# Two-block transformer kernel, MLP: the odd parts' up activations turned by sixteen VectorE transposes

## The chip, the cores and the metric

One core of a Trainium2 chip runs the whole program. The metric is the device time of one execution in microseconds (us); for the kernel before it is the median of three runs.

## The reference, cut to what matters

Two transformer blocks run on 256 tokens of width 2048 in float32. The change lies in the MLP of the first block only, which is

```python
h = rmsnorm(x, norm_mlp_g[l])
x = x + jnp.square(jax.nn.relu(h @ w_up[l])) @ w_down[l]      # 2048 -> 8192 -> 2048
```

## The kernel before, in words

Every float32 weight is split into a high and a low fp32r part, so that a product is three TensorE products (high x high, low x high, high x low). Weights come in **units** of 128 x 1024 numbers (512 KB). SyncE loads a unit into one of four slots of `w_raw`, ScalarE copies it rounded to `w_hi` (`split`, line 1273), VectorE subtracts to get `w_lo` (`split`, line 1989), and TensorE runs twelve 128 x 512 products on it (`token_unit`, line 636). ScalarE and VectorE work four units ahead: in step `j` of their loops they split unit `j + 4`, which ScalarE may do once TensorE is through with unit `j`, because it takes the same slot.

The MLP is cut into 16 parts of 512 hidden columns. A part's up projection is a chunk of 8 units; its down projection is 4 chunks of 2 units, one for each 512 output columns. Two PSUM sets take turns from chunk to chunk. After a chunk, VectorE adds the set to `x` (`add_tokens`, line 2004, two instructions) and so frees it; the down chunks are 2 units long, so that the set is wanted again two units after the chunk's end. Seven passes of one loop, counted 0 to 6 here, do two parts each in 32 steps: units 0 to 7 up (part `2i+1`), 8 to 15 down (part `2i`), 16 to 23 up (part `2i+2`), 24 to 31 down (part `2i+1`). The adds stand in steps 9, 11, 13, 15, 25, 27, 29 and 31.

TensorE's up products have the tokens on the partitions; the down products want the hidden columns there. So a part's activations are turned: ScalarE applies relu and square (lines 1469 and 1472, in step 7 for the odd part, semaphore `hid_sq`), VectorE transposes the blocks of 32 x 32 in place of quadrants by one instruction (`turn_blocks`, line 2338, step 10), and ScalarE moves the sixteen groups of blocks to their quadrants of 32 partitions (`move_blocks`, shown in the profile at line 1273 as `arena<-arena 32x256`, two in each of steps 11 to 18). Then ScalarE and VectorE make the high and the low part (`moved_hi` in step 20, `moved_lo` in step 21, line 2343), on which the down units wait (`hid_ready`).

The same VectorE queue also multiplies the modulation weights of the second block (`ada`, line 1984, `arena<-arena,cs 128x768`) in every step of 0 to 23 but each third. Step 28 sums them up (`partial_sums`, `modulation`). GpSimd builds tables beside this; its three stages are released by `hid_ready` (waits on line 3144 and after), so they begin after a `moved_lo`.

Engines take their instructions strictly in the order of the code. The feed-forward stage of the second block already turns its product in quadrant pieces on VectorE (`turn_product`, line 2941), two in each of eight steps.

Of the kernel before, what the change touches and what calls it, by code (L numbers as in the profile page):

```python
# [38 lines left out]
FT = COLS // P  # L39
# [249 lines left out]
def two_blocks(nc, a, consts, columns, x_by_dim, s5_in, s5_blocks, small_in, wide_in2, out):  # L289
# [5 lines left out]
    sem = {n: ctx.enter_context(nc.semaphore(n)) for n in SEMS}  # L295
# [56 lines left out]
    def vec(name, i=0, n=1):  # L352
        g, r, k = VEC[name]
        return vecs[:, g * P + r + i:g * P + r + i + n]

    def T(t, n=None):
        return arena[:, t, :] if n is None else arena[:, t:t + n, :]

    def flat(ap):
        return ap.rearrange("p a b -> p (a b)")  # L360
# [41 lines left out]
    def span(t, off, n):  # L402

        return arena[:, :, :].rearrange("p a b -> p (a b)")[:, t * S + off:t * S + off + n]
# [15 lines left out]
    HID_B, HID_T = 4, 8  # L420
# [6 lines left out]
    def by_block(tiles):  # L427

        return flat(tiles).rearrange("p (t f g b) -> p t f g b", t=TT, f=FT, g=QUADS)

    def by_feature(tiles):

        return tiles.rearrange("p f (t g b) -> p t f g b", t=TT, g=QUADS)

    def quad(q):

        return slice(q * QUAD, (q + 1) * QUAD)
# [833 lines left out]
    def _(act):  # L1271
        def copy(o, i, scale=1.0):
            return nc.scalar.activation(o, i, ACT.Copy, scale=scale)  # L1273

        def split(R, j, first=False, cols=COLS):

            act.wait_ge(raw_landed[j % RAW], (R * (8 // RAW) + j // RAW) * 16 + 16)
            if not first:
                act.wait_ge(sem["unit_done"], R * 8 + (j - LEAD + 1))
            copy(w_hi[:, j % LEAD, :, 0:cols], w_raw[:, j % RAW, :, 0:cols]).then_inc(sem["hi_ready"], 1)  # L1280
# [6 lines left out]
        def halves(ap):  # L1287
            return ap.rearrange("p (a b) -> p a b", a=2)
# [67 lines left out]
        for b in range(KT // 2):  # L1356
# [3 lines left out]
            for k in range(2 * b, 2 * b + 2):  # L1360
                m = copy(hop_hi[:, k], T(XT + k), scale=vec("norm_mix_g", k))
# [72 lines left out]
        for j in range(4 * UA):  # L1434
# [16 lines left out]
            for c in range(3):  # L1451
                if j == OUT_LAST[c] + 1:
                    i = OUT_GROUPS.index((c, 1))
# [20 lines left out]
        def move_blocks(m, first, n):  # L1474

            act.wait_ge(sem["hid_turned"], m + m + 1)
            for k in range(first, first + n):
                q, g = k // QUADS, k % QUADS
                i = copy(by_feature(T(HID_T, FT))[quad(g), :, :, q], by_block(T(HID_B, FT))[quad(q), :, :, g])
            if first + n == QUADS * QUADS:  # L1480
                i.then_inc(sem["hid_turned"], 1)

        def moved_hi(par, m):

            act.wait_ge(sem["hid_turned"], m + m + 2)
            copy(hid_hi[:, par], T(HID_T, FT)).then_inc(sem["hid_hi"], 1)
# [22 lines left out]
        with act.Fori(0, MLP_SUPER // 2 - 1) as i:  # L1509
            for j in range(4 * UA):  # L1510
                split(R_MLP + 1 + 4 * i, j + LEAD)
                if j in (4, 20):
                    moved_hi(j // 20, 2 * i + j // 20)
                if j < 3:
                    move_blocks(2 * i, 10 + 2 * j, 2)
                if 11 <= j < 19:
                    move_blocks(2 * i + 1, 2 * (j - 11), 2)
                if 27 <= j < 32:
                    move_blocks(2 * i + 2, 2 * (j - 27), 2)
                if j == 7:  # L1520
                    hidden_relu(1, H_MLP + 5 * i, 2 * i + 1)
                if j == 23:
                    hidden_relu(0, H_MLP + 5 * i + 3, 2 * i + 2)
# [140 lines left out]
        for h in range(BR_HEADS):  # L1664
            c = 4 + h
            for q in range(UA):
                projection_unit(c, q)
                wide_lo(c, q)
                if q in (1, 2):
                    m = q - 1  # L1670
                    act.wait_ge(sem["d_negmax"], 2 * h + m + 1)
                    e = span(34, CW * m, CW)
                    for qt, cols in enumerate((slice(0, P), slice(P, CW))):
                        i = nc.scalar.activation(e[:, cols], e[:, cols], ACT.Exp, bias=st[:, 0, 2 * m + qt:2 * m + qt + 1],
                                                 accum_out=st[:, 1, 2 * m + qt:2 * m + qt + 1])
# [37 lines left out]
        for h in range(BR_HEADS):  # L1713
            c = 8 + h
            for q in range(UA):
# [10 lines left out]
                if h == 0 and q == 1:  # L1726
                    act.wait_ge(sem["g_z_psum"], 1)
                    for t in range(2):
                        m = nc.scalar.activation(T(8 + t), PS[4][:, t * S:(t + 1) * S], ACT.Identity, bias=vec("gla_ba_2", t))
                    m.then_inc(sem["g_z"], 1)  # L1730
                    head_root(0, 34)
                if q == 3:
# [3 lines left out]
                    for qt, cols in enumerate((slice(0, P), slice(P, CW))):  # L1736
                        m = nc.scalar.activation(e[:, cols], e[:, cols], ACT.Exp, bias=st[:, 0, 2 + qt:3 + qt])
# [74 lines left out]
        for i in range(4):  # L1812
            source = (0, 4, 0, 24)[i]
            for j in range(40):
# [8 lines left out]
                if j % 10 == 7:  # L1823
                    n = j // 10
# [10 lines left out]
                    for t in range(TT):  # L1835
                        m = nc.scalar.activation(flat(o)[:, t * COLS:(t + 1) * COLS], SETS[0][t][:], ACT.Sigmoid)
# [4 lines left out]
                if i == 3 and j in (13, 23, 33):  # L1841
                    n = j // 10 - 1
                    act.wait_ge(sem["merged_turned"], n + 1)
                    act.wait_ge(sem["hid_ready"], MLP_SUPER + 4)
                    for b in range(2):
                        m = copy(T(16 + FT * n + 2 * b, 2), halves(PS[5 + b][:]))
# [7 lines left out]
        def mix_square(c, t, junk):  # L1854

            return nc.scalar.activation(junk, SETS[c % 2][t][:], ACT.Square, accum_out=sums[:, SUM_MIX, t, c:c + 1])
# [10 lines left out]
        for j in range(4 * UA - LEAD):  # L1867
# [5 lines left out]
            if j % UA == UA - 1:  # L1873
                c = j // UA
                for t in range(TT):
                    m = mix_square(c, t, span(24, t * COLS, COLS))
# [64 lines left out]
        R, m = R_FFN + 2 + 6 * PAIRS, 2 * PAIRS + MLP_SUPER  # L1941
# [31 lines left out]
    def _(dve):  # L1973
        V = nc.vector
# [98 lines left out]
        for b in range(KT // 2):  # L2073
            dve.wait_ge(sem["hop_hi"], 2 * (b + 1))
            for k in range(2 * b, 2 * b + 2):
                m = stt(hop_lo[:, k], T(XT + k), vec("norm_mix_g", k), hop_hi[:, k].bitcast(F32), ALU.mult, ALU.subtract)
# [176 lines left out]
        for j in range(8 * UA):  # L2253
# [16 lines left out]
            if j == 12:  # L2270
                token_inverse(1, SUM_X)
                dve.wait_ge(sem["const_in"], 16)
                for t in range(TT):
                    m = V.tensor_scalar(span(46, t * P, P), ident, inverse(SUM_X, t), None, ALU.mult)
# [60 lines left out]
        def turn_blocks(m):  # L2335

            dve.wait_ge(sem["hid_sq"], m + 1)
            V.transpose(flat(T(HID_B, FT)), flat(T(0, FT))).then_inc(sem["hid_turned"], 1)  # L2338

        def moved_lo(par, m):  # L2340

            dve.wait_ge(sem["hid_hi"], m + 1)
            V.tensor_tensor(hid_lo[:, par], T(HID_T, FT), hid_hi[:, par].bitcast(F32), ALU.subtract).then_inc(sem["hid_ready"], 1)

        turn_blocks(0)
        with dve.Fori(0, MLP_SUPER // 2 - 1) as i:
            R, H = R_MLP + 1 + 4 * i, H_MLP + 5 * i
            for j in range(4 * UA):
                split(R, j + LEAD)
                if j in (5, 21):  # L2350
                    moved_lo(j // 21, 2 * i + j // 21)
                down_ends(R, j, 8, 0, x_tok)
                down_ends(R, j, 24, 1, x_tok)
                ada(ADA_ONE, j, i + G_MLP)
                if j in (10, 26):
                    turn_blocks(2 * i + (1 if j == 10 else 2))
                if j == 28:
                    partial_sums(i + G_MLP)
                    modulation(i + G_MLP)
# [36 lines left out]
        for j in range(3 * UA - LEAD):  # L2396
# [11 lines left out]
            if j in (17, 19):  # L2408
                n = j // 19
                dve.wait_ge(drained[n], H_IN2)  # L2410
                for t in range(TT):
                    m = gained(t, n)
# [90 lines left out]
        for j in range(3 * UA + SMALL_UNITS):  # L2503
# [7 lines left out]
            if 4 <= j < 8:  # L2511
                c = j - 4
                for t in range(TT):
                    m = V.tensor_scalar(x_tok[:, t, part(c)], Y_TOK[:, t, part(c)], inverse(SUM_MID, t), None, ALU.mult)
# [124 lines left out]
        for h in range(BR_HEADS):  # L2639
            for q in range(UA):  # L2640
# [16 lines left out]
                if h == 2 and q == 5:  # L2657
# [5 lines left out]
                    for t in range(2):  # L2663
                        m = V.tensor_tensor_scan(run[:, t, 1:S + 1], ones[:, 0:1].to_broadcast([P, S]), la[:, t], 0.0,
                                                 ALU.mult, ALU.add)
# [140 lines left out]
        for i in range(4):  # L2806
            R, H = R_GATE + 5 * i, H_GATE + 4 * i
            source = (0, 4, 0, 24)[i]
            for j in range(40):
# [7 lines left out]
                if j % 10 == 9:  # L2817
                    n = j // 10
# [3 lines left out]
                    for b in range(2):  # L2822
                        m = V.tensor_tensor(sig[:, 2 * b:2 * b + 2], halves(SETS[1][b][:]), sig[:, 2 * b:2 * b + 2], ALU.mult)
# [39 lines left out]
        for j in range(4 * UA - LEAD):  # L2863
# [14 lines left out]
            if j % UA == UA - 1:  # L2878
# [3 lines left out]
                for t in range(TT):  # L2882
                    m = gained_mix(c, t)
# [381 lines left out]
```

## Time and profile before

| what | value |
|---|---|
| median of 3 runs | 2606.64 us (2604.88 to 2607.6) |
| the profiled execution | 2607.81 us |
| its span | 2605.8 us |
| TensorE products (PE) busy | 2570.9 us, 99% |
| VectorE (DVE) busy | 2023.2 us, 78% |
| ScalarE (ACT) busy | 1360.8 us, 52% |
| granted TensorE clock | 0.997 of full |

The span is the time between the first and the last instruction of the profiled execution. Busy shares are of the span; matmuls overlap one another, so their busy time is not that of TensorE at its peak. Which engine ends the waits of the others is read from the rows on single stretches.

### The profile page before, as it was taken

The numbers are of one execution on the slowest core, as the hardware profiler recorded it, in microseconds if no ns is written. First come the engines' busy times: TensorE is split into PE (matmuls) and PEld (weight loads), VectorE is DVE, ScalarE is ACT, GpSimd is POOL, SyncE is SP. The second block draws the span as 40 slices with busy tenths as digits, with TensorE's granted clock in tenths as the row PEclk, the third lists the DMA queues.
The fourth block names the chain that finished last, engine by engine and source line by source line (L and its number), as shares of the span: only waits on it lengthen the run. The fifth ranks groups of instructions, "written<-read, shape, count | busy, mean of one in ns | idle before, by whom it ended". The sixth has DMA issues, their size and how long they took to land.

```text
span 2605.8 us, 35123 instructions
## 1 busy us (share of the span) xinstructions
PE 2570.9 (99%) x12360; PEld 2145.7 (82%) x12360; DVE 2023.2 (78%) x2572; ACT 1360.8 (52%) x1774; POOL 277.3 (11%) x309
## 2 busy tenths in 40 slices
PE   9999999999999999999999999999999999999998
PEld 8998888888878887888888877888788888888886
DVE  5798778888888879876676888787866666666798
ACT  6445565656565656455556444444544444444444
POOL 0021042233222000071000000000000000000000
PEclk9999999999999999999999999999999999999999
DMA  9666687879787886756555766789566666666785
GB/s 314 225 209 228 223 284 254 275 259 310 248 281 262 306 274 212 277 170 222 170 173 162 258 226 212 240 304 323 181 202 193 193 193 193 193 193 193 258 298 187
DMA packets 284076, 611.10 MB, mean 235 GB/s; under 512 B 20400, under 2 KB 21620, under 8 KB 282048
## 3 DMA queue, kind: packets, MB, share of 16 engines
q1 hardware_dynamic: 279104, 583.54, 68.6%
q0 software_dynamic: 4864, 26.14, 2.8%
q8 instruction: 66, 1.08, 0.2%
q14 instruction: 42, 0.34, 0.0%
HBM read 599.08 MB, written 11.29 MB: 234 GB/s over the span
## 4 chain that ended last, share of the span: by engine, by line
PE 87%; DVE 7%; issue 3%; ACT 3%; DMA 1%; DVEq 0%; SPq 0%; ACTq 0%
PE ps L636 86%; DVE w_lo L1989 1%; DVE arena L1984 1%; ACT w_hi L1273 1%; DMA w_raw<-in_w_in 1%; DVE x L2004 0%; DVE hop_part L1984 0%; PE ps L756 0%; DVE arena L2941 0%; DMA w_raw<-in_ffn_w_out 0%; ACT hop_part L1273 0%; PE ps L777 0%; DVE arena L2004 0%; DVE mod_parts L2115 0%; DVE x L1984 0%
## 5 line engine op out<-in xcount | busy, mean ns | idle before, releaser
L1273 ACT ACTIVATE w_hi<-w_raw 128x1024 fp32r<-128x1024 f32 (+1 forms) x898 | 948.1, 1057 | 1153.1 <-PE ps L636 1040.8
L1989 DVE TENSOR_TENSOR w_lo<-w_raw,w_hi 128x1024 fp32r<-128x1024 f32 x809 | 1014.2, 1255 | 476.1 <-ACT w_hi L1273 472.3
L636 PE MATMUL ps<-w_hi,hop_part 128*128 128x512 f32 x4264 | 1334.5, 391 | 3.4 <-DVE w_lo L1989 1.5
L636 PEld LDWEIGHTS ps<-w_hi,hop_part 128*128 128x128 f32 x4264 | 800.7, 188 | 178.1 <-issue 8.3
L636 PE MATMUL ps<-w_lo,hop_part 128*128 128x512 f32 x2132 | 829.8, 389 | 0.0
L636 PEld LDWEIGHTS ps<-w_lo,hop_part 128*128 128x128 f32 x2132 | 400.5, 188 | 81.4
L636 PE MATMUL ps<-w_hi,hid_hi_part 128*128 128x512 f32 x992 | 387.5, 391 | 2.8 <-DVE x L2004 2.7
L636 PE MATMUL ps<-w_hi,hid_lo_part 128*128 128x512 f32 x992 | 386.0, 389 | 0.0
L636 PE MATMUL ps<-w_lo,hid_hi_part 128*128 128x512 f32 x992 | 386.0, 389 | 0.0
L636 PE MATMUL ps<-hop_part,w_hi 128*128 128x256 f32 (+1 forms) x1312 | 275.3, 333 | 5.8 <-DVE hop_part L1984 5.8
L1984 DVE SCALAR_TENSOR_TENSOR arena<-arena,cs 128x768 f32<-128x768 f32 x240 | 254.7, 1061 | 0.3
L636 PEld LDWEIGHTS ps<-hop_part,w_hi 128*128 128x128 f32 x1312 | 216.5, 194 | 25.1 <-issue 7.6
L636 PEld LDWEIGHTS ps<-w_hi,hid_hi_part 128*128 128x128 f32 x992 | 186.2, 188 | 45.0 <-issue 6.3
L636 PEld LDWEIGHTS ps<-w_hi,hid_lo_part 128*128 128x128 f32 x992 | 186.2, 188 | 38.8
L636 PEld LDWEIGHTS ps<-w_lo,hid_hi_part 128*128 128x128 f32 x992 | 186.3, 188 | 38.1
L636 PE MATMUL ps<-hop_part,w_lo 128*128 128x256 f32 x912 | 176.6, 284 | 0.0
L2489 DVE TENSOR_TENSOR w_lo<-w_raw,w_hi 128x1024 fp32r<-128x1024 f32 x84 | 106.1, 1267 | 61.9 <-ACT w_hi L1273 61.6
L636 PEld LDWEIGHTS ps<-hop_part,w_lo 128*128 128x128 f32 x912 | 143.7, 192 | 5.2
L1273 ACT ACTIVATE arena<-arena 32x256 f32<-32x256 f32 x240 | 99.8, 416 | 19.3 <-DVE arena L2338 15.4
L2004 DVE TENSOR_TENSOR x<-ps,x 128x512 f32<-128x512 f32 x124 | 79.3, 680 | 0.0
L3173 POOL DMA_DIRECT2D gain_scratch<-arena x2 | 1.0, 520 | 678.8 <-ACT arena L1273 678.8
L636 PE MATMUL ps<-arena 64*128 64x128 f32 (+4 forms) x496 | 69.3, 342 | 3.8 <-DVE arena L2177 2.9
(320 smaller groups left out, 1424.2 us busy)
## 6 DMA issues: line engine op xcount, KB each, us to landing
arena<-in_ada_w SPq DMA_DIRECT2D x256, 384.0 KB, 5.1
w_raw<-in_ffn_w_in SPq DMA_DIRECT2D x176, 512.0 KB, 3.7
w_raw<-in_w_up SPq DMA_DIRECT2D x128, 512.0 KB, 4.2
w_raw<-in_w_down SPq DMA_DIRECT2D x128, 512.0 KB, 4.8
w_raw<-in_w_gate SPq DMA_DIRECT2D x128, 512.0 KB, 4.3
w_raw<-in_ffn_w_out SPq DMA_DIRECT2D x88, 512.0 KB, 3.6
w_raw<-in_w_in SPq DMA_DIRECT2D x87, 512.0 KB, 4.3
w_raw<-in_w_out SPq DMA_DIRECT2D x64, 512.0 KB, 5.5
```

Source lines behind the costliest of these rows:

```text
L636: return nc.tensor.matmul(o, w, r, start=start, stop=stop, skip_group_check=True)
L1273: return nc.scalar.activation(o, i, ACT.Copy, scale=scale)
L1984: return V.scalar_tensor_tensor(o, i0, scalar, i1, op0, op1, **k)
L1989: V.tensor_tensor(w_lo[:, j % LEAD, :, 0:cols], w_raw[:, j % RAW, :, 0:cols], w_hi[:, j % LEAD, :, 0:cols].bitcast(F32), ALU.subtract).the ...
L2004: m = V.tensor_tensor(at[:, t, part(c)], SETS[s][t][:], at[:, t, part(c)], ALU.add)
L2489: V.tensor_tensor(w_lo[:, slot], w_raw[:, slot], w_hi[:, slot].bitcast(F32), ALU.subtract).then_inc(sem["lo_ready"], 1)
L3173: pool.dma_start(gain_scratch[i].rearrange("(k p) -> k p", p=P), gain_rows[32 + 32 * i:32 + 32 * i + KT, :]).then_inc(sem["scratch_out"], 16)
```

## The change

In steps 10 to 17 of the loop, VectorE issues two transposes of 32 partitions x 256 elements after whatever else the step holds. Each reads one quadrant of the squared activations `T(0, FT)` and writes the quadrant of `T(HID_T, FT)` to which the blocks belong. The one block instruction of step 10 and ScalarE's sixteen moves in steps 11 to 18 go. The last piece raises `hid_turned` by 2, for the block instruction and for the last move. The even parts keep the old way (`turn_blocks` in step 26, `move_blocks` in steps 27 to 31 and 0 to 2 of the next pass), as does the part before the loop, and the last part is turned by TensorE as before. Nothing on TensorE, SyncE or GpSimd changes.

```diff
@@ ScalarE's loop
                 if j < 3:
                     move_blocks(2 * i, 10 + 2 * j, 2)
-                if 11 <= j < 19:
-                    move_blocks(2 * i + 1, 2 * (j - 11), 2)
                 if 27 <= j < 32:
                     move_blocks(2 * i + 2, 2 * (j - 27), 2)
@@ VectorE
+        def turn_piece(m, n):
+
+            dve.wait_ge(sem["hid_sq"], m + 1)
+            q = n // 2
+            for g in range(2 * (n % 2), 2 * (n % 2) + 2):
+                i = V.transpose(by_feature(T(HID_T, FT))[quad(g), :, :, q], by_block(T(0, FT))[quad(q), :, :, g])
+            if n == 7:
+                i.then_inc(sem["hid_turned"], 2)
@@ VectorE's loop
                 ada(ADA_ONE, j, i + G_MLP)
-                if j in (10, 26):
-                    turn_blocks(2 * i + (1 if j == 10 else 2))
+                if j == 26:
+                    turn_blocks(2 * i + 2)
+                if 10 <= j < 18:
+                    turn_piece(2 * i + 1, j - 10)
```

On VectorE, steps 10 to 13 of the loop stand like this before (each step begins with the `w_lo` row; `x<-ps,x` is the add of a chunk, `arena<-arena,cs` the modulation product):

```order
L1989 TENSOR_TENSOR w_lo<-w_raw,w_hi 128x1024
L2108 REGISTER_ALU
L1984 SCALAR_TENSOR_TENSOR arena<-arena,cs 128x768
L2337 REGISTER_ALU
L2338 STREAM_TRANSPOSE arena<-arena 128x1024
L1988 REGISTER_ALU
L1989 TENSOR_TENSOR w_lo<-w_raw,w_hi 128x1024
L2004 TENSOR_TENSOR x<-ps,x 128x512 x2
L1988 REGISTER_ALU
L1989 TENSOR_TENSOR w_lo<-w_raw,w_hi 128x1024
L2102 ISA
L2108 REGISTER_ALU
```

The changed kernel has, from the same `w_lo` row of step 10 on:

```order
L1987 TENSOR_TENSOR w_lo<-w_raw,w_hi 128x1024
L2106 REGISTER_ALU
L1982 SCALAR_TENSOR_TENSOR arena<-arena,cs 128x768
L2340 REGISTER_ALU
L2343 STREAM_TRANSPOSE arena<-arena 32x2x4x32 x2
L1986 REGISTER_ALU
L1987 TENSOR_TENSOR w_lo<-w_raw,w_hi 128x1024
L2002 TENSOR_TENSOR x<-ps,x 128x512 x2
L2343 STREAM_TRANSPOSE arena<-arena 32x2x4x32 x2
L1986 REGISTER_ALU
L1987 TENSOR_TENSOR w_lo<-w_raw,w_hi 128x1024
```

One large transpose in step 10 has become a pair of small ones there and a pair behind the add of step 11; further pairs close each step up to 17, so that three pairs stand ahead of the add of step 13.

On ScalarE, the steps from 11 on before:

```order
L1273 ACTIVATE w_hi<-w_raw 128x1024
L1476 REGISTER_ALU
L1273 ACTIVATE arena<-arena 32x2x4x32 x2
L1277 ISA
L1279 REGISTER_ALU
L1273 ACTIVATE w_hi<-w_raw 128x1024
L1273 ACTIVATE arena<-arena 32x2x4x32 x2
```

and in the changed kernel:

```order
L1273 ACTIVATE w_hi<-w_raw 128x1024
L1277 ISA
L1279 REGISTER_ALU
L1273 ACTIVATE w_hi<-w_raw 128x1024
L1279 REGISTER_ALU
L1273 ACTIVATE w_hi<-w_raw 128x1024
```

The moves between the high splits are gone, and with them the wait for `hid_turned` that stood ahead of the first of them.

## Rows read from the trace of the kernel before

**Rows 1.** The page, busy time of each engine: engine, busy us (share) xinstructions.

```profile
PE   2570.9 (99%) x12360; PEld 2145.7 (82%) x12360; DVE 2023.2 (78%) x2572; ACT 1360.8 (52%) x1774; POOL 277.3 (11%) x309
```

**Rows 2.** Stretches: sum us, busy PE, PEld, DVE, ACT, POOL, PEclk, DMA share, GB/s.

```profile
441.76:465.49 23.73, 22.36 (x98) 17.87 (x96) 23.73 (x22) 13.94 (x19) 9.64 (x6) 1.00 0.88 316
531.34:553.10 21.76, 21.76 (x97) 18.02 (x96) 20.71 (x22) 13.94 (x19) 6.23 (x5) 1.00 0.85 280
574.86:596.62 21.76, 21.76 (x97) 18.02 (x96) 21.35 (x27) 13.94 (x19) 10.55 (x7) 1.00 0.75 258
618.38:640.14 21.76, 21.76 (x97) 18.02 (x96) 20.68 (x22) 13.94 (x19) 20.03 (x35) 1.00 0.86 280
```

**Rows 3.** Timeline of PE, pass 1: start us, us, instruction [idle before <-releaser].

```profile
452.41 0.39 PE L636 MATMUL ps<-w_hi,hid_lo_part 128*128 128x512 f32 x1
453.45 0.49 PE L636 MATMUL ps<-w_hi,hid_hi_part 128*128 128x512 f32 x1 [0.65 <-DVE x L2004]
453.78 0.39 PE L636 MATMUL ps<-w_lo,hid_hi_part 128*128 128x512 f32 x1
```

**Rows 4.** Timeline of DVE: adds of steps 9, 11, 13 of pass 1, 13 of pass 3.

```profile
452.05 1.27 DVE L2004 TENSOR_TENSOR x<-ps,x 128x512 f32<-128x512 f32 x2
...
458.50 1.27 DVE L2004 TENSOR_TENSOR x<-ps,x 128x512 f32<-128x512 f32 x2
...
462.94 1.28 DVE L2004 TENSOR_TENSOR x<-ps,x 128x512 f32<-128x512 f32 x2
...
637.34 1.27 DVE L2004 TENSOR_TENSOR x<-ps,x 128x512 f32<-128x512 f32 x2
```

**Rows 5.** Groups: busy us, mean ns of one, idle ahead: the ScalarE moves.

```profile
L1273 ACT ACTIVATE arena<-arena 32x256 f32<-32x256 f32 x240 | 99.8, 416 | 19.3 <-DVE arena L2338 15.4
```

**Rows 6.** Timeline of DVE, feed-forward stage: pieces in steps without idle time.

```profile
2446.40 1.23 DVE L1989 TENSOR_TENSOR w_lo<-w_raw,w_hi 128x1024 fp32r<-128x1024 f32 x1 [0.36 <-ACT w_hi L1273]
2447.54 0.87 DVE L2941 STREAM_TRANSPOSE arena<-arena 32x256 f32<-32x256 f32 x2
2448.43 0.62 DVE L2106 TENSOR_SCALAR arena<-arena,cs 128x768 f32<-128x768 f32 x1
2449.12 1.23 DVE L1989 TENSOR_TENSOR w_lo<-w_raw,w_hi 128x1024 fp32r<-128x1024 f32 x1
2450.37 0.89 DVE L2941 STREAM_TRANSPOSE arena<-arena 32x256 f32<-32x256 f32 x2
2451.28 1.02 DVE L1984 SCALAR_TENSOR_TENSOR arena<-arena,cs 128x768 f32<-128x768 f32 x1
```

**Rows 7.** Timeline of DVE, pass 2: steps 10, 11 and 13.

```profile
543.40 1.24 DVE L2338 STREAM_TRANSPOSE arena<-arena 128x1024 f32<-128x1024 f32 x1
544.57 1.18 DVE L1989 TENSOR_TENSOR w_lo<-w_raw,w_hi 128x1024 fp32r<-128x1024 f32 x1
545.67 1.28 DVE L2004 TENSOR_TENSOR x<-ps,x 128x512 f32<-128x512 f32 x2
...
550.10 1.28 DVE L2004 TENSOR_TENSOR x<-ps,x 128x512 f32<-128x512 f32 x2
551.30 1.01 DVE L1984 SCALAR_TENSOR_TENSOR arena<-arena,cs 128x768 f32<-128x768 f32 x1
552.22 1.22 DVE L1989 TENSOR_TENSOR w_lo<-w_raw,w_hi 128x1024 fp32r<-128x1024 f32 x1
```

**Rows 8.** Timeline of DVE, pass 2: step 21, then 23 to 25, then 29.

```profile
570.71 1.23 DVE L1989 TENSOR_TENSOR w_lo<-w_raw,w_hi 128x1024 fp32r<-128x1024 f32 x1 [1.50 <-ACT w_hi L1273]
...
577.62 6.29 DVE L1989 TENSOR_TENSOR w_lo<-w_raw,w_hi 128x1024 fp32r<-128x1024 f32 x3
583.83 1.27 DVE L2004 TENSOR_TENSOR x<-ps,x 128x512 f32<-128x512 f32 x2
...
594.95 1.28 DVE L2004 TENSOR_TENSOR x<-ps,x 128x512 f32<-128x512 f32 x2
```

**Rows 9.** DMA issues in the loop, 325 to 1000 us: KB each, us to landing.

```profile
w_raw<-in_w_up SPq DMA_DIRECT2D x116, 512.0 KB, 4.2
```

## Prediction

> **What bounds the kernel now.** I read the busy times first: TensorE's products fill 99% of the span, VectorE's work 78% [rows 1]. So the change can only matter where TensorE waits, or comes to wait, in the stretch it touches. The second view is the table of stretches [rows 2]. Its first, third and fourth columns of time show the length, TensorE's and VectorE's work. Eight units take TensorE 21.76 us when nothing disturbs it, 2.72 us a unit, at a granted clock of 1.00. In the down units of step 8 to 15 VectorE is busy 20.71 of 21.76 us in pass 2 and 20.68 in pass 3; in pass 1 it is busy for the whole stretch, and the stretch has grown to 23.73 us (pass 4 reads the same). So here VectorE stands a few tenths of a us behind the bound, while ScalarE has 8 us to spare (13.94 of 21.76).
>
> The third view is the timeline around the two waits of pass 1 [rows 3, 4]. The product at 452.41 us should be followed 0.23 us later, at 452.64, but the next begins at 453.45, and the profile names the add to x as releaser. The add of step 9 began at 452.05 and took 1.27, so ended at 453.32. The product behind the wait is a long one (0.49 in place of 0.39), and the next comes at 453.78, as if the first had begun at 453.55. So a chunk costs TensorE nothing as long as the add that frees its PSUM set ends 0.23 us ahead of its start, and each us later costs a us. Here the loss is 453.32 + 0.23 - 452.64 = 0.91 us. The add of step 11 ended at 459.77; two units behind 453.55 is 458.99, so it cost 1.01. Together 1.92, and the stretch is 1.97 longer: the rule accounts for it.
>
> What reaches the end of the program is therefore the end of the adds. In pass 2 the add of step 13 begins at 550.10 [rows 7] and ends at 551.38, and unit 16, which wants its set, starts at 553.10: it has 1.72 - 0.23 = 1.49 us to spare.
>
> **What the change removes.** ScalarE loses 16 moves of 416 ns in each of seven passes [rows 5], 46.6 us. I price this at nothing: with 8 us of 21.76 idle, ScalarE is behind TensorE's release of a slot, not ahead of it. VectorE loses one block transpose in each pass. From its start to that of the step 11 add are 2.27 us, with one split between [rows 7]; a split is 1.14 us from start to start [rows 6], so the block transpose is worth 1.13.
>
> **What it adds.** The feed-forward stage has the same pieces, in a place without idle time [rows 6]. The first pair, 2447.54 to 2448.43, holds VectorE for 0.89 us, and the split ahead of it keeps its 1.14. The second stands 1.25 us behind its split's start, and the next instruction 0.91 after the pair's: the split's end no longer overlaps what follows, which is 0.11 more. So the first pair (both pieces read quadrant 0, the first also writes it) costs 0.89, every other 0.91 + 0.11 = 1.02. These rows show the 0.11 behind a split alone; in steps 11 to 13 the pairs stand behind an add or a modulation product. Those two also overlap their followers: an add takes 1.28 and the next starts after 1.20, a product 1.01 and 0.92 [rows 7]. I take 1.02 there too; the other bound is 0.91.
>
> By the Trainium skill, page "VectorE: DVE Perf Modes", section "Two Vector instructions with no wait between them", an instruction that starts in another quadrant than the last one read or wrote is held until all earlier ones have finished. By it the sum is the one below, since every pair but the first is held whatever stands ahead of it; were it held behind splits alone, the sum would be the second case's. Rows 6 agree with it, 1.14 us behind a split for the first pair and 1.25 for the next.
>
> **The add of step 13.** The pair in step 10 replaces the block transpose: the add of step 11 starts 0.89 + 1.14 = 2.03 us after it, 0.24 earlier. Then two more pairs, 2.04, stand ahead of the add of step 13, so it comes 1.80 us later. In pass 2: 550.10 + 1.28 + 1.80 + 0.23 = 553.41 against 553.10, a loss of 0.31 where there was none. I take passes 0, 5 and 6 like it: 1.24. In pass 3 the add starts at 637.34 and takes 1.27 [rows 4]; with 2.03 more that is 640.64 against 640.14 [rows 2], 0.50. In passes 1 and 4 the loss at step 11 shrinks by 0.24, unit 16 would start at 465.49 - 0.24 = 465.25, and the add of 462.94 ends at 464.22, with 2.03 more 466.25: 1.00 lost, 0.76 net; 1.52 for both. The add of step 15 has a whole chunk of 8 units to spare. Sum: 1.24 + 0.50 + 1.52 = 3.26 us.
>
> **The splits behind it.** All eight pairs cost 0.89 + 7 x 1.02 = 8.03. From the start of step 10's pair to that of step 17's split stand seven pairs (7.01), six splits (6.84), three adds (3.60) and four modulation products (3.68): 21.13 us. In pass 2 that split starts at 564.53, its result counts from 564.53 + 1.23 + 0.23 = 565.99, and unit 21 is due at 553.41 + 5 x 2.72 = 567.01. One us is left; the loads stay covered too: unit 25's, released by it at 565.76, lands 4.2 us later [rows 9], 569.96, and ScalarE has until 571.95 to split it, when VectorE comes for it (next part).
>
> **What VectorE takes on into the second half.** From the block transpose (543.40) to step 21 (570.71) are 27.31 us [rows 7, 8]. The work in them is 2.27 + nine splits 10.26 + three adds 3.60 + six products 5.52 = 21.65, so 5.66 are idle. The change adds 8.03 - 1.13 = 6.90, and 1.24 stay over. Most passes lose that in idle stretches behind it. Not passes 2 and 5: there GpSimd begins its longest step after `moved_lo`, and the three splits of steps 23 to 25 take 6.29 us in place of 3.4, with no idle time up to the add of step 25 [rows 8]. That add ends at 583.83 + 1.27 + 1.24 + 0.23 = 586.57 by the rule; unit 28 is due at 574.86 + 10.88 + 0.31 = 586.05: 0.52 lost. The add of step 29 comes to 596.23 + 1.24 + 0.23 = 597.70 against 596.62 + 0.31 + 0.52 = 597.45, 0.25 more. Two passes: 1.54 us.
>
> **Sum.** 3.26 + 1.54 = 4.8 us more. The profiled execution took 2607.81 us and would take 2612.6; the median of the runs is 1.17 below it, so 2606.64 + 4.8 = 2611.4 us, 0.18% more. A measurement of this kernel can tell about 0.2%, or 5.2 us, from no change.
>
> **The rivals.**
>
> First, *pairs held only behind splits*. Pairs in steps 11 and 12 cost 0.91, the add of step 13 is 0.22 earlier: losses of 0.09 in four passes, 0.28 in pass 3, 0.54 in passes 1 and 4, 1.72 in all. VectorE keeps 5 x 0.11 less, 0.69; the adds of steps 25 and 29 then lose 0.19 and 0.25, twice 0.44. Total 2.6, so 2609.2 us. For it: I have no row of a pair behind an add. Against: each piece in rows 6 but the first starts after its forerunner's full duration.
>
> Second, *slower: GpSimd stretches the pieces too*. Pass 3 has it busy for 20.03 of 21.76 us [rows 2], pass 0 is in the same stage of the tables. Were pieces stretched as the splits of rows 8, 6.29 / 3.42 = 1.84 times, three pairs ahead of the step 13 add would be 3 x 0.89 x 0.84 = 2.2 us longer, in two passes 4.5: 9.3 in all, 2615.9 us. It decides against "no difference" from 0.2 us in each of the two passes on. Against: the add of pass 3 takes 1.27 us [rows 4], as in pass 1 where GpSimd has finished, so not every VectorE instruction is stretched. A late load ends on the same side: one that takes over a us longer than in rows 9 shifts steps 21 to 25 of passes 2 and 5 by the rest.
>
> Third, *faster, by ScalarE's freedom*. ScalarE waited 15.4 us for the block transposes [rows 5]; without that its splits come earlier. But TensorE lost only 1.97 us in such a stretch, to adds, not to splits, and all that the change can return there is 0.24 us in each of two passes if the step 13 add still fits: 2606.2 us. Faster by over 0.2% has no source.
>
> **How the numbers follow.** The forecast, 4.8 us with its own spread of 3.5 to 6.5, has 50%; pairs held only behind splits or mostly hidden (under 3.5) 24%; stretched pieces or late loads (over 6.5) 24%; faster 2%. The range of 8 in 10 goes from 2608.3, just under the second case, to 2615.9, the stretched one. A third of the forecast's own share lies over 5.2 us, so slower by over 0.2% has 0.17 + 0.24 = 0.41; within 0.2% 0.57; faster 0.02.
>
> **What would show it.** Stretches of pass 2 and 6 of about 22.1 us from unit 8 to 16 with a wait for `x` at unit 16; of passes 1 and 4 of 24.5; a first wait at unit 28 in passes 2 and 5; pairs of 0.87 to 0.89 us that start only after their forerunner's full duration; ScalarE's busy time 46.6 us lower, VectorE's 7 x (8 x 0.89 - 1.24), about 41 us, higher. Wrong is the prediction if TensorE waits for `w_lo` (splits, not adds, were the limit), if pieces take over 0.5 us, or if the waits are there and the time doesn't follow.

## The result, and the profile after

The changed kernel takes 2611.04 us (median of 22 runs, 2609.73 to 2613.91), the kernel before 2606.61 us (22 runs, 2604.68 to 2609.34) on the same chip. The ratio is 1.0018, with a 95% interval of 1.0012 to 1.0024: 0.18% slower, just inside the 0.2% that a measurement of this kernel can tell from no change. The forecast was 2611.4 us.

The busy times of the page after, to be read beside [rows 1]: engine, busy us, share of the span, instructions.

```profile
PE 2572.4 (99%) x12360; PEld 2144.1 (82%) x12360; DVE 2063.2 (79%) x2677; ACT 1314.4 (50%) x1662; POOL 277.0 (11%) x309
```

ScalarE's work is 46.4 us less (46.6 forecast) and VectorE's 40.0 us more (about 41 forecast). TensorE's own is the same but for 1.5 us, so the time went into waits. The list of waits between 325 and 1000 us of the span says for what: engine and line, awaited engine and line, us in total, times, longest.

```profile
PE ps L636 <- DVE x L2002: 5.6, 12, 0.7
```

Before, the same list had 3.3 us in 6 waits for `x`, and both have one more of 0.5 us for `w_lo` ahead of the loop. So in the loop the list still names adds to x alone; no wait for a split has come. It names only 2.3 us more than before, since it leaves out short waits and counts idle time from the modelled end of a product (0.39 us), not from the 0.23 us after which the next would start. Counted from one product's start to the next, the waits and the products right behind them hold 4.8 of the 5.06 us by which the loop (below) has grown.

The table of stretches of the kernel after, with the columns of [rows 2]. First pass 1 from unit 8 to 16 and from 16 to 24, then the four stretches of eight units from pass 2's unit 8 on.

```profile
441.71:466.07 24.36, 22.51 (x98) 17.68 (x96) 24.21 (x26) 11.25 (x12) 9.64 (x6) 1.00 0.86 308
466.07:487.97 21.90, 21.90 (x96) 18.12 (x97) 21.59 (x28) 8.79 (x9) 0.70 (x3) 1.00 0.79 253
531.97:553.92 21.95, 21.92 (x97) 17.84 (x96) 20.75 (x26) 10.61 (x11) 6.24 (x5) 1.00 0.83 271
553.92:575.83 21.91, 21.91 (x97) 18.12 (x98) 21.60 (x28) 9.45 (x9) 0.71 (x1) 1.00 0.78 255
575.83:598.30 22.47, 21.92 (x98) 17.84 (x96) 22.12 (x28) 14.46 (x20) 11.75 (x7) 1.00 0.81 278
598.30:620.18 21.88, 21.88 (x97) 18.12 (x97) 16.55 (x16) 12.25 (x17) 1.64 (x4) 1.00 0.91 313
```

Stretches that were 21.76 us [rows 2] are now 21.95 to 22.47, and pass 1's 23.73 is 24.36. Each wait leaves 0.12 to 0.15 us in the stretch behind it too (21.91 and 21.88 where 21.76 would do), most of it because the first product after a wait is the long one of 0.49 us. So the 22.1 and 24.5 us that the prediction gave as signs for pass 2 and pass 1 read 21.95 and 24.36. For that reason the clearest measure is a whole pass, from the first product of its unit 8 to that of the next pass. Summed over seven passes I call it the loop. It was 614.48 us before (354.59 to 969.07) and is 619.54 after (354.00 to 973.54): 5.06 us more, where the forecast had 4.8. Outside the loop the two profiled executions differ by 0.59 us one way before it and 0.60 the other way behind it, which no step of the change touches. The kernels of the experiments, with the same code ahead of the loop, reach it anywhere between 351.62 and 354.59 us. So a whole execution scatters by more than the loop does, and the medians (4.43 us apart) and the loop (5.06) need not agree to half a us.

| pass, us | 0 | 1 | 2 | 3 | 4 | 5 | 6 | loop |
|---|---|---|---|---|---|---|---|---|
| before | 87.17 | 89.58 | 87.04 | 87.04 | 89.57 | 87.04 | 87.04 | 614.48 |
| after | 87.71 | 90.26 | 88.21 | 87.53 | 90.24 | 88.23 | 87.36 | 619.54 |
| difference | 0.54 | 0.68 | 1.17 | 0.49 | 0.67 | 1.19 | 0.32 | 5.06 |
| forecast | 0.31 | 0.76 | 1.08 | 0.50 | 0.76 | 1.08 | 0.31 | 4.80 |

The timeline of TensorE after, at the waits of pass 1, the start of unit 16 of pass 2, and its unit 32 (columns as in [rows 3]):

```profile
453.40 0.49 PE L636 MATMUL ps<-w_hi,hid_hi_part 128*128 128x512 f32 x1 [0.65 <-DVE x L2002]
...
466.07 0.49 PE L636 MATMUL ps<-w_hi,hop_part 128*128 128x512 f32 x1 [0.69 <-DVE x L2002]
...
553.51 0.39 PE L636 MATMUL ps<-w_hi,hid_lo_part 128*128 128x512 f32 x1
553.92 0.49 PE L636 MATMUL ps<-w_hi,hop_part 128*128 128x512 f32 x1
...
598.30 0.49 PE L636 MATMUL ps<-w_hi,hop_part 128*128 128x512 f32 x1 [0.55 <-DVE x L2002]
```

Pass 1 keeps its wait at step 9's add, loses a little of the second (0.50 at 459.63, where it was 0.72) and gets a new one at unit 16, 0.69. In pass 2 the product of 553.51 should be followed at 553.74 and is followed at 553.92 by a long one. This wait is too short for the view to name a releaser, but it is there: 0.18 us, and 0.10 more in the long product.

The other half of the picture is VectorE, pass 2, steps 10 to 13 (beside [rows 7]; the frame of this execution lies 0.63 us later, since pass 2's unit 8 starts at 531.97 where it was 531.34):

```profile
544.04 0.87 DVE L2343 STREAM_TRANSPOSE arena<-arena 32x256 f32<-32x256 f32 x2
544.92 1.23 DVE L1987 TENSOR_TENSOR w_lo<-w_raw,w_hi 128x1024 fp32r<-128x1024 f32 x1
546.07 1.28 DVE L2002 TENSOR_TENSOR x<-ps,x 128x512 f32<-128x512 f32 x2
547.38 0.89 DVE L2343 STREAM_TRANSPOSE arena<-arena 32x256 f32<-32x256 f32 x2
548.28 1.23 DVE L1987 TENSOR_TENSOR w_lo<-w_raw,w_hi 128x1024 fp32r<-128x1024 f32 x1
549.42 1.01 DVE L1982 SCALAR_TENSOR_TENSOR arena<-arena,cs 128x768 f32<-128x768 f32 x1
550.47 0.88 DVE L2343 STREAM_TRANSPOSE arena<-arena 32x256 f32<-32x256 f32 x2
551.37 1.23 DVE L1987 TENSOR_TENSOR w_lo<-w_raw,w_hi 128x1024 fp32r<-128x1024 f32 x1
552.51 1.28 DVE L2002 TENSOR_TENSOR x<-ps,x 128x512 f32<-128x512 f32 x2
```

The second pair starts 1.31 us after the add's start (1.28 long, it would free its follower after 1.20), the third 1.05 after the modulation product's (1.01 long, 0.92). So the overlap of 0.1 us is lost behind adds and products just as behind splits. There is no idle time in these rows. The add of step 13 stands at 552.51, in the frame of before 551.88: 1.78 us later than 550.10, where 1.80 was forecast.

### The profile page after: what moved, and what is told of

The parts are those of the page before. It is cut to its first block, busy times and chain, and to the rows that moved or that the text cites. A ratio compares the mean times of both kernels' runs of the same rounds, so it can differ in the third digit from the quotient of the medians.

```text
span 2610.9 us, 35109 instructions
## 1 busy us (share of the span) xinstructions
PE 2572.4 (99%) x12360; PEld 2144.1 (82%) x12360; DVE 2063.2 (79%) x2677; ACT 1314.4 (50%) x1662; POOL 277.0 (11%) x309
## 3 DMA queue, kind: packets, MB, share of 16 engines
q8 instruction: 66, 1.08, 0.2%
## 4 chain that ended last, share of the span: by engine, by line
PE 80%; DVE 10%; issue 5%; ACT 3%; DMA 2%; DVEq 0%; SPq 0%; ACTq 0%
PE ps L636 80%; DVE w_lo L1987 3%; DVE arena L1982 2%; DVE x L2002 1%; ACT w_hi L1273 1%; DMA w_raw<-in_w_in 1%; DVE arena L2343 1%; DMA w_raw<-in_w_gate 1%; DVE hop_part L1982 0%; PE ps L756 0%; DMA w_raw<-in_w_down 0%; ACT hop_part L1273 0%; PE ps L777 0%; DVE arena L2749 0%; DVE mod_parts L2113 0%
## 5 line engine op out<-in xcount | busy, mean ns | idle before, releaser
L2950 DVE STREAM_TRANSPOSE arena<-arena 32x256 f32<-32x256 f32 x160 | 69.7, 436 | 3.3
```

What stands on the lines that cost most here:

```text
L2950: m = V.transpose(by_feature(T(PROD_T, FT))[quad(g), :, :, q], by_block(T(20, FT))[quad(q), :, :, g])
```

## Experiments

Each ratio is to the kernel before on the same chip, with a 95% interval, from 11 runs of each kernel (4 of the one with each piece twice). The loop is from the one profiled execution.

| kernel | median, us | ratio | loop, us | against after's loop |
|---|---|---|---|---|
| ScalarE's moves gone, rest as before | 2605.94 | 0.9997 (0.9988 to 1.0006) | 614.50 | -5.04 |
| pieces within quadrant 0 | 2605.71 | 0.9995 (0.9986 to 1.0004) | 614.05 | -5.49 |
| no piece in step 12 | 2608.95 | 1.0010 (1.0001 to 1.0019) | 616.80 | -2.74 |
| each piece twice | 2644.08 | 1.0145 (1.0129 to 1.0160) | 652.72 | +33.18 |
| sums in step 30 | 2608.75 | 1.0012 (1.0003 to 1.0021) | 617.38 | -2.16 |
| no piece in step 12, sums in step 30 | 2606.28 | 0.9998 (0.9989 to 1.0007) | 614.32 | -5.22 |
| before, sums in step 30 | 2604.90 | 0.9994 (0.9985 to 1.0003) | 613.32 | -6.22 |

The passes of the kernels, us from unit 8 to unit 8, are the rows by which they are told apart:

| pass | 0 | 1 | 2 | 3 | 4 | 5 | 6 |
|---|---|---|---|---|---|---|---|
| moves gone | 87.18 | 89.59 | 87.03 | 87.04 | 89.58 | 87.04 | 87.04 |
| within quadrant 0 | 87.17 | 89.34 | 87.04 | 87.03 | 89.39 | 87.04 | 87.04 |
| no piece in step 12 | 87.35 | 89.43 | 88.21 | 87.12 | 89.43 | 88.22 | 87.04 |
| each piece twice | 92.24 | 94.67 | 93.45 | 92.22 | 94.67 | 93.47 | 92.00 |
| sums in 30 | 87.91 | 89.79 | 87.38 | 87.50 | 90.08 | 87.35 | 87.37 |
| both edits | 87.25 | 89.21 | 87.25 | 87.13 | 89.18 | 87.26 | 87.04 |
| before, sums in 30 | 87.17 | 88.99 | 87.04 | 87.04 | 89.00 | 87.04 | 87.04 |

### The half of the change that takes work from ScalarE

From the kernel before, the sixteen moves of the odd parts are left out, so the blocks of these parts don't reach their place; VectorE's side is as before, with the count that the waits behind it want.

```diff
-                if 11 <= j < 19:
-                    move_blocks(2 * i + 1, 2 * (j - 11), 2)
...
-            V.transpose(flat(T(HID_B, FT)), flat(T(0, FT))).then_inc(sem["hid_turned"], 1)
+            V.transpose(flat(T(HID_B, FT)), flat(T(0, FT))).then_inc(sem["hid_turned"], count)
```

> The kernel before with ScalarE's sixteen moves of each odd part left out and nothing in their place; the block transpose of step 10 stays and raises hid_turned by 2. The odd parts' high and low parts are then made of what the tile held, so the output is not the reference's. Theory of the adds: ScalarE's moves were off the path, so the time is that of before within 0.3 us, all four waits of passes 1 and 4 at units 12 and 14 stay, 46.6 us of ScalarE's busy time go. Rival, ScalarE's freedom gives back something that the pieces then more than eat: 1 to 3 us faster than before. Second rival, the rest of the change is slower because ScalarE's splits now come at other times: slower than before by 1 us or more here.

TensorE's waits for x between 325 and 1000 us:

```profile
PE ps L636 <- DVE x L2002: 3.3, 6, 0.7
```

ScalarE is busy for 1314.3 us, 46.5 less than before, and TensorE's waits are the 3.3 us in 6 of the kernel before; every pass is within 0.01 us of it. ScalarE's freedom returns nothing to TensorE: the whole result of the change comes from VectorE's side.

### The hold between quadrants

The number, size and place of the pieces stay; each now reads and writes quadrant 0 alone (the turned activations land in the wrong place).

```diff
-                i = V.transpose(by_feature(T(HID_T, FT))[quad(g), :, :, q], by_block(T(0, FT))[quad(q), :, :, g])
+                o = T(32 + 4 * q + g)[quad(0), :].rearrange("p (t f b) -> p t f b", t=TT, f=FT)
+                i = V.transpose(o, by_block(T(0, FT))[quad(0), :, :, g])
```

> The changed kernel with all sixteen pieces reading quadrant 0 and writing quadrant 0 of sixteen spare tiles, so nothing is turned across quadrants and the output is not the reference's. As many pieces of the same size, in the same steps. Theory that most of the price of a pair is that every piece waits for the full end of what stands ahead: pieces overlap by 0.08 us each as other instructions do, a pair costs 0.7 us in place of 1.02, the add of step 13 comes 1.0 us later than before in place of 1.8 and fits into the 1.49 us to spare, and VectorE carries nothing into the second half: 2606.6 us, no wait at unit 16 of passes 0, 2, 3, 5, 6. Rival, a piece costs what it costs wherever it reads and writes: 2611.0 us and all the waits of the changed kernel.

Timeline of VectorE, pass 2, steps 10 and 11:

```profile
543.08 1.17 DVE L1987 TENSOR_TENSOR w_lo<-w_raw,w_hi 128x1024 fp32r<-128x1024 f32 x1
544.18 1.27 DVE L2002 TENSOR_TENSOR x<-ps,x 128x512 f32<-128x512 f32 x2
545.38 0.74 DVE L2344 STREAM_TRANSPOSE arena<-arena 32x256 f32<-32x256 f32 x2
546.07 1.17 DVE L1987 TENSOR_TENSOR w_lo<-w_raw,w_hi 128x1024 fp32r<-128x1024 f32 x1
```

A pair now holds VectorE for 0.69 us, starts 1.20 after the add in place of 1.31, and the split behind it also comes 0.04 sooner (1.10 in place of 1.14 or 1.15). From the add of step 11 to that of step 13 (549.89 here) are 5.71 us in place of 6.44, with two pairs between: 0.36 us a pair are gone, and all of TensorE's losses with them: passes 0, 2, 3, 5 and 6 are those of before, passes 1 and 4 are even 0.2 shorter, because the add of step 11 comes earlier. Not all of the 0.36 is the hold itself: a piece that stays in its quadrant is also shorter (404 ns in the median of 112, against 436). The same instructions in the same places cost nothing when they stay within one quadrant, so the price of the change is that of changing the quadrant, laid on a VectorE with 1.5 us to spare. This also dismisses a cost of the count of instructions or of the waits around them.

### No piece in step 12

The piece ahead of the add of step 13 moves behind it.

```diff
-                if 10 <= j < 18:
-                    turn_piece(2 * i + 1, j - 10)
+                if j in (10, 11) or 13 <= j < 19:
+                    turn_piece(2 * i + 1, j - 10 - (j > 12))
```

> The changed kernel with the pair of step 12 and all behind it one step later (pairs in steps 10, 11 and 13 to 18): the same work, one pair less ahead of the add of step 13. Theory of the adds: that add comes 1.02 us earlier, the waits at unit 16 go in passes 0, 2, 3, 5 and 6 (1.7 us) and shrink to the 0.2 us gained at unit 14 in passes 1 and 4 (2 x 1.0 us); what VectorE carries over to passes 2 and 5's second half stays, 1.6 us. So 3.7 us less than the changed kernel, 2607.3 us, 0.7 to 1.1 more than before. Rival, VectorE's whole load between steps 10 and 20 decides and not the place ahead of the add: 2611 us, with the lost time later in the pass.

The table of stretches, pass 2 from unit 8 to 16 and from 24 to 32:

```profile
528.62:550.38 21.76, 21.76 (x98) 18.02 (x96) 20.58 (x25) 10.60 (x11) 6.22 (x5) 1.00 0.87 271
...
572.14:594.92 22.78, 22.11 (x97) 17.69 (x96) 22.43 (x28) 14.56 (x20) 12.07 (x7) 1.00 0.84 279
```

The wait at unit 16 is gone as expected. But the loop gave back 2.74 us, not 3.7. Passes 2 and 5 explain two thirds of the difference: they take 88.21 and 88.22 us, to 0.01 what they take in the changed kernel. The loss of 0.34 at unit 16 went, and the one at unit 32 grew from 0.83 to 1.17. The adds of the second half come when VectorE's backlog lets them, and a TensorE that wasn't delayed at unit 16 meets them with the whole delay. So in those two passes the two losses of the forecast are not two costs in a sum, but one, 1.17 us, of which the first wait pays a part in advance. I hadn't said that, though the numbers of the forecast contain it: they put unit 32 at 597.70 whatever unit 16 loses.

The same holds on a smaller scale in passes 0, 1, 3 and 4, at unit 24, which wants `moved_lo`. In pass 1 `moved_lo` begins 44.19 us after unit 8, as in the changed kernel (483.38 against 439.19, there 485.90 against 441.71), but TensorE comes sooner: its first product of unit 24 is a long one at 484.73, 0.13 after `moved_lo` has ended. Such waits cost about 0.1 us in passes 0 and 3 and up to 0.4 in passes 1 and 4, and the list of waits leaves them out.

### Each piece twice

Each piece is issued a second time into another tile.

```diff
-                i = V.transpose(by_feature(T(HID_T, FT))[quad(g), :, :, q], by_block(T(0, FT))[quad(q), :, :, g])
+                for tile in (HID_B, HID_T):
+                    i = V.transpose(by_feature(T(tile, FT))[quad(g), :, :, q], by_block(T(0, FT))[quad(q), :, :, g])
```

> The changed kernel with every piece issued twice, the first time into the tile of the block transpose, which is free in those steps: a dose. The output stays the reference's. Theory of the adds and, past their reserve, of VectorE's load: a step with a pair is 0.88 us longer; the add of step 13 comes 2.64 us later, all of it lost, and by step 17 the splits themselves are the limit: TensorE waits for w_lo at units 21 and 22, 2.5 and 1.0 us more. 6.2 us for each of seven passes and 1 to 2 us in the second halves of passes 2 and 5: 45 us over the changed kernel, 2656 us (2645 to 2665). Rival, the losses come from single accidental waits and don't grow with VectorE's load: under 2625 us.

TensorE's waits between 325 and 1000 us, and then VectorE's timeline at step 10 of pass 2:

```profile
PE ps L636 <- DVE x L2002: 19.0, 13, 2.2
PE ps L636 <- DVE w_lo L1987: 6.2, 13, 0.7
PE ps L636 <- DVE hid_lo_part L2351: 5.1, 7, 0.7
```

```profile
550.80 1.52 DVE L2344 STREAM_TRANSPOSE arena<-arena 32x256 f32<-32x256 f32 x4
552.34 1.23 DVE L1987 TENSOR_TENSOR w_lo<-w_raw,w_hi 128x1024 fp32r<-128x1024 f32 x1
```

The loop grows by 33.2 us where 45 was expected, and the median misses the foot of my range by 1 us. The reason stands in the rows: four pieces take 1.54 us from start to the next start, not 2 x 0.88. The second copy reads and writes the quadrants of the first, and is not held. One step costs 0.65 more; 56 steps make 36.4, and 33.2 of it reached TensorE. So once VectorE has no slack, nine tenths of what is put on it are paid. The splits and `hid_lo` come late as well, for which the list of the changed kernel names no wait in the loop. I had put 3.5 us a pass on the splits; the list names 5.7 us for them in all seven passes (0.5 of the 6.2 lies ahead of the loop).

### The sums two steps later

The partial sums and the modulation stand in step 28, ahead of the add of step 29. They move behind it.

```diff
-                if j == 28:
+                if j == 30:
                     partial_sums(i + G_MLP)
```

> The changed kernel with partial_sums and modulation in step 30 in place of step 28, so behind the add of step 29. In the trace of the changed kernel TensorE waits for that add at unit 32: 0.8 us in passes 2 and 5, 0.4 to 0.5 in passes 1 and 4. If those waits are what the second halves lose, they go: 2.5 us less than the changed kernel, 2608.5 us. Rival, what VectorE is behind is only met at another place (the add of step 31, or unit 8 of the next pass): 2611 us.

The table of stretches, pass 2: unit 8 to 16, and 24 to 32.

```profile
531.55:553.50 21.95, 21.92 (x97) 17.84 (x96) 20.75 (x26) 10.61 (x11) 6.23 (x5) 1.00 0.81 266
...
575.41:597.17 21.76, 21.76 (x98) 18.02 (x96) 20.39 (x18) 13.94 (x19) 11.75 (x7) 1.00 0.84 276
```

The wait at unit 32 is gone in passes 1, 2, 4 and 5, and that of unit 16 stays: pass 2 loses 0.34, pass 5 0.31. The loss of the second half is thus shown to be the add of step 29 behind a backlog, with the sums as the last piece of it. The loop gave back 2.16 of the expected 2.5 us. Pass 0 has taken 0.2 more than in the changed kernel, which began ahead of the loop (a wait for `hid_lo_part` of 0.33 at 353.85). Pass 4 has taken 0.29 more than pass 1, and there a late load is paid for. ScalarE in pass 4:

```profile
749.26 1.06 ACT L1273 ACTIVATE w_hi<-w_raw 128x1024 fp32r<-128x1024 f32 x1 [2.54 <-DMA w_raw<-in_w_down]
```

This load landed 5.71 us after its issue, where the same load took 3.98 in the changed kernel. VectorE then sat idle for 0.78 us before the split, `moved_lo` began 45.07 us after unit 8 in place of 44.19, and the first product of unit 24 is a long one at 752.84, 0.13 after `moved_lo` has ended.

### Both edits, and the kernel before with the sums moved

The first has both diffs above, the second only the move of the sums, made in the kernel before.

> The changed kernel with both edits: pairs in steps 10, 11 and 13 to 18, sums and modulation in step 30. By the theory of the adds only the waits of passes 1 and 4 at units 12 and 14 and a small one at unit 16 stay: 2605.0 us, 1.6 under before, 6 under the changed kernel. Rival, the two edits' gains overlap, since VectorE's load is the same: 2607 or more.

> The kernel before with sums and modulation in step 30. Only the two waits at unit 32 of passes 1 and 4 can go, 0.57 us each: 2605.5 us, 1.1 under before. If e6 is not faster than this one, the pieces on VectorE bring nothing of their own even in their best place; the theory says e6 is 0.5 us faster by the shorter wait at unit 14.

The table of stretches of the kernel with both edits: pass 1 from unit 8 to 16 and 16 to 24, then pass 2 from unit 24 to 32.

```profile
440.61:464.12 23.51, 22.36 (x97) 17.85 (x96) 23.42 (x24) 10.60 (x11) 9.64 (x6) 1.00 0.86 312
464.12:486.15 22.03, 21.98 (x97) 17.85 (x97) 21.66 (x29) 9.46 (x9) 0.07 (x2) 1.00 0.77 248
...
573.34:595.31 21.97, 21.97 (x98) 17.87 (x96) 20.66 (x18) 13.92 (x19) 12.07 (x7) 1.00 0.82 276
```

The kernel before with the sums moved came as expected: its loop is 1.16 us shorter, for 1.1. With both edits the change costs nothing against the kernel before (0.9998, loop 0.16 us shorter), but the expectation was 1.6 us less than before, and less than the other by 0.5. It isn't: the kernel before with the sums moved has the shorter loop by 1.00 us and the lower median by 1.4. By medians neither of the two is told from the kernel before: both intervals hold 1.

The 0.20 us that pass 1 gains up to unit 16 (23.51 us for 23.71 in the kernel before with the sums moved, since the add of step 11 comes earlier) is lost in the stretch behind, 22.03 for 21.76, and pass 2 has 0.21 more from unit 24 to 32. The list of waits names nothing for either, but the timelines do, by the long product of 0.49 us that comes behind a wait. VectorE and TensorE at unit 24 of pass 1, then at unit 30 of pass 2:

```profile
484.80 1.22 DVE L2350 TENSOR_TENSOR hid_lo_part<-arena,hid_hi_part 128x1024 fp32r<-128x1024 f32 x1
486.15 0.49 PE L636 MATMUL ps<-w_hi,hid_hi_part 128*128 128x512 f32 x1
...
588.33 1.27 DVE L2002 TENSOR_TENSOR x<-ps,x 128x512 f32<-128x512 f32 x2
589.73 0.49 PE L636 MATMUL ps<-w_hi,hid_hi_part 128*128 128x512 f32 x1
```

Both products start 0.13 us after the instruction of VectorE has ended, as those do whose releaser the view names. So unit 24 of pass 1 waited for `moved_lo`, again 44.19 us after unit 8, and unit 30 of pass 2 for the add of step 27. The second of these is 0.12 of the 0.21 us. The backlog that the pieces leave is still there; with the larger waits gone TensorE meets it at other places, in part as the rival of this run had it.

## Why the prediction was right

**The bound and the rule.** TensorE's lost time in the loop is waits for adds that free a PSUM set. The rule, an add's end plus 0.23 us, puts unit 16 of pass 2 at 552.51 + 1.28 + 0.23 = 554.02; it began at 553.92 with a long product, as if at 554.02. At unit 32 the add of 596.86 gives 598.37 against 598.30 and the same 0.10. The forecast had 597.70 there in the frame of before, 598.33 in this one.

**Removed: the moves, at nothing.** Shown by the kernel without them.

**Added: 1.02 for a held pair.** I had taken it for pairs behind adds and products too, without a row for it. The rows of steps 10 to 13 show it, and the kernel within quadrant 0 shows what the hold is worth: without it nothing is lost. This is also the end of the first rival, pairs held only behind splits. The rule that I took from the Trainium skill, page "VectorE: DVE Perf Modes", section "Two Vector instructions with no wait between them", is borne out by both: an instruction that changes the quadrant starts 0.03 us after the end of a split, add or product and 0.01 after that of a piece, one that doesn't 0.06 to 0.08 ahead of the end.

**The add of step 13.** 1.78 us later for 1.80. The losses at unit 16 were 0.32 to 0.34 in passes 2, 5 and 6 (0.31), 0.49 in pass 3 (0.50), 0.77 in passes 1 and 4 (0.76). Pass 0 lost 0.54, 0.23 over the forecast. Taking it like pass 2 looked safe, as its own add left 1.47 us in the kernel before. But here that add comes 1.97 us later, counted from unit 8, in part because the adds of steps 11 and 13 are 6.60 us apart in place of 6.44. One split between them takes 1.34 for 1.23, and a modulation product 1.05 for 1.01:

```profile
373.62 1.34 DVE L1987 TENSOR_TENSOR w_lo<-w_raw,w_hi 128x1024 fp32r<-128x1024 f32 x1
```

GpSimd is busy for 20.55 of the 22.28 us there. So there may be a little of the second rival in it, on other instructions than the pieces; that GpSimd is the cause is not tested.

**The splits, with a us to spare.** Step 17's split stands at 565.17, in the frame of before 564.54, where 564.53 was forecast. TensorE waited for none.

**The second half: size right, place wrong.** The forecast had 0.52 at unit 28 and 0.25 at unit 32 of passes 2 and 5. There was no wait at unit 28; the whole loss came at unit 32. VectorE after, pass 2, from `moved_lo` on (beside [rows 8], again 0.63 later):

```profile
573.76 1.22 DVE L2350 TENSOR_TENSOR hid_lo_part<-arena,hid_hi_part 128x1024 fp32r<-128x1024 f32 x1
...
575.83 1.21 DVE L1987 TENSOR_TENSOR w_lo<-w_raw,w_hi 128x1024 fp32r<-128x1024 f32 x1
576.96 1.79 DVE L1982 SCALAR_TENSOR_TENSOR arena<-arena,cs 128x768 f32<-128x768 f32 x1
578.68 6.27 DVE L1987 TENSOR_TENSOR w_lo<-w_raw,w_hi 128x1024 fp32r<-128x1024 f32 x3
584.88 1.27 DVE L2002 TENSOR_TENSOR x<-ps,x 128x512 f32<-128x512 f32 x2
586.07 2.23 DVE L1987 TENSOR_TENSOR w_lo<-w_raw,w_hi 128x1024 fp32r<-128x1024 f32 x1
...
596.86 1.28 DVE L2002 TENSOR_TENSOR x<-ps,x 128x512 f32<-128x512 f32 x2
```

The same stretch of VectorE in the kernel before:

```profile
571.86 1.22 DVE L2343 TENSOR_TENSOR hid_lo_part<-arena,hid_hi_part 128x1024 fp32r<-128x1024 f32 x1
...
573.92 2.06 DVE L1989 TENSOR_TENSOR w_lo<-w_raw,w_hi 128x1024 fp32r<-128x1024 f32 x1
...
585.03 1.21 DVE L1989 TENSOR_TENSOR w_lo<-w_raw,w_hi 128x1024 fp32r<-128x1024 f32 x1
```

`moved_lo` comes 1.27 later in its frame (573.76 - 0.63 against 571.86), where 1.24 was forecast. But what VectorE loses beside GpSimd's long step doesn't shift as a block with it. GpSimd before and after:

```profile
573.22 1.68 POOL L3134 TENSOR_TENSOR arena<-arena,s5pow_im 128x512 f32<-128x512 f32 x1 [35.41 <-DVE hid_lo_part L2343]
...
575.12 2.82 POOL L3143 TENSOR_TENSOR arena<-arena,s5pow_im 128x512 f32<-128x512 f32 x1 [36.68 <-DVE hid_lo_part L2350]
```

The step begins 1.27 later too, but now its first instruction is the longer one, and the split beside it is not stretched (1.21 for 2.06, 0.85 less). So the add is late by 0.42 only and ends at 586.15, 0.33 before the rule bites (unit 28 at 575.83 + 10.88 = 586.71). The split behind the add is stretched instead (2.23 for 1.21), and by the add of step 29 the delay is 1.28. The step that failed is "that add ends at 583.83 + 1.27 + 1.24": I moved the add by the whole backlog, as if the stretched instructions stayed the same. It cost the sum nothing, since the last wait of the half collects all of it; the experiments without the first wait and with the sums moved both show this. That the delay would be whole again by the add of step 29 (1.28 for 1.24), after a smaller one at step 25, I had not worked out; there the size came right by luck.

**The rivals.** Stretched pieces did not come. The 112 pieces of all passes, by line (count: min, median, max in ns, first and last start), were never stretched, in pass 0 and 3 with GpSimd busy for 20 us of 22 neither. But in no run did a piece stand beside a GpSimd step of 128x512 elements, as the stretched splits of [rows 8] did; what that would do to a piece is open.

```profile
L2343 DVE STREAM_TRANSPOSE arena<-arena x112: 425/436/442, 366.2 to 921.1; 32x256 f32<-32x256 f32 x112
```

The other half of this rival, late loads, had one sentence. The loads took hardly longer in the median (4.1 us for the up weights and 5.0 for the down weights, before 4.2 and 4.8), but ScalarE came to wait for them. Its waits for loads between 325 and 1000 us, after (before they were 3.7 us in 3 and 1.7 us in 2):

```profile
ACT w_hi L1273 <- DMA w_raw<-in_w_down: 27.9, 19, 2.0
ACT w_hi L1273 <- DMA w_raw<-in_w_up: 8.2, 4, 2.7
```

These are 36.1 us in place of 5.4. The part for the up weights goes with ScalarE's freedom: it is 7.7 us with the moves gone alone. The part for the down weights goes with VectorE's lateness: 3.4 us with the moves gone, 3.6 within quadrant 0, 10.5 without a piece in step 12, 27.9 here and 62.1 with each piece twice. That a later split of VectorE releases the slot later is my explanation and fits this, but no run tests it alone. In the changed kernel the waits cost TensorE nothing that shows, as no wait of it names a split; the run with the sums in step 30 has one that cost 0.29 us. Faster by ScalarE's freedom: dead as well, by the kernel without moves.

## What to carry to other kernels

An engine that is 78% busy on average may have only 1.5 us to spare in one place: count the work between the last slack and the instruction that frees what the bound wants, and judge each new instruction by whether it stands ahead of that one or behind it. Here the third pair ahead of the add cost TensorE 0.3 to 0.8 us a pass in five of the seven passes. Moved behind the add, it left these five within 0.2 us of the kernel before. Waits that come of one backlog don't add up: removing the first hands its share to the next, so price the backlog at the last of them, and look for waits too short for the list of waits. Moving work off an engine with idle time gained nothing here; what it costs on the other is measured where that one is fullest.

## What the runs showed of the hardware

A pair of 32x256 transposes costs 1.02 us of VectorE when its pieces change the quadrant and 0.69 when they don't; part of this is in the piece itself, 404 ns for 436. A piece that repeats its forerunner's quadrants is not held either, four take 1.54. Beside a GpSimd step of 128x512 elements VectorE's two-input instructions on SBUF are mostly longer: in the changed kernel, from 340 to 1000 us, 18 splits wholly beside such a step took 2.06 us in the median and 215 beside none 1.23; the modulation product took 1.80 for 1.01. The four instructions of adds, which read PSUM, took 0.68 us as elsewhere. Sometimes it is GpSimd's instruction that grows instead (2.82 for 1.68), beside a split of 1.21. And a wait of TensorE costs 0.10 us beyond the idle time, in a first product of 0.49 us whose follower comes after 0.33. That product shows a wait even where it is too short for the view to name a releaser.
